# A five-layer transformer kernel: modulation vectors by a multiply-and-sum along rows of 1024 on VectorE instead of sums over partitions

## What is computed

```python
c_act = jax.nn.silu(c)
for i in range(DEPTH):
    mod = c_act @ ada_w[i] + ada_b[i]                    # [1024] @ [1024, 6144]
    sh1, sc1, g1, sh2, sc2, g2 = jnp.split(mod, 6, axis=-1)
    h = modulate(rmsnorm(x, norm_gain[i, 0]), sh1, sc1)
    y = mixer(h)                                         # swa, gla or fox
    x = x + g1[:, None, :] * y
    h = modulate(rmsnorm(x, norm_gain[i, 1]), sh2, sc2)
    x = x + g2[:, None, :] * swiglu(h, ffn_w_gu[i], ffn_w_down[i])
```

## Time and profile before

| | us |
|---|---|
| median of 3 runs | 1900.2 |
| lowest, highest | 1897.8, 1906.18 |
| span of the profiled execution (first to last instruction) | 1892.6 |
| median less that span | 7.6 |
| PE busy in the profiled execution | 1724.5 |
| DVE busy | 1362.8 |
| ACT busy | 813.9 |
| POOL busy | 630.0 |
| mean granted clock of PE, of full speed | 0.924 |

### The profile page before, as it was taken

One profiled execution on the slowest core, in us unless ns is written; L12 is line 12 of the kernel. 1 busy time (PEld: TensorE's weight loads), 2 busy tenths in 40 slices (PEclk: granted clock), 3 DMA queues, 4 the chain that ended last, 5 costly groups with the idle time before them and its releaser, 6 DMA issues.

```text
span 1892.6 us, 32608 instructions
## 1 busy us (share of the span) xinstructions
PE 1724.5 (91%) x12934; PEld 1603.9 (85%) x12934; DVE 1362.8 (72%) x1665; ACT 813.9 (43%) x1113; POOL 630.0 (33%) x268
## 2 busy tenths in 40 slices
PE   2868899989899999899999998989999898799998
PEld 2836899989789999897699998859999787489998
DVE  6886899986647999843259998855999854535554
ACT  2333444445534433443343443454344355445453
POOL 0112244532102544321224544133454314314433
PEclk9967899989889999897599999969999999799999
DMA  9642588764314876642048876404887635125551
GB/s 351 263 142 84 223 352 305 275 266 163 129 67 189 350 291 259 255 168 89 1 157 333 300 293 241 164 1 156 331 309 291 242 136 190 34 95 178 193 179 44
DMA packets 53937, 382.71 MB, mean 202 GB/s; under 512 B 6224, under 2 KB 6480, under 8 KB 8160
## 3 DMA queue, kind: packets, MB, share of 16 engines
q1 hardware_dynamic: 51840, 375.23, 52.6%
q0 software_dynamic: 2016, 6.36, 1.0%
HBM read 377.37 MB, written 4.19 MB: 202 GB/s over the span
## 4 chain that ended last, share of the span: by engine, by line
issue 40%; PE 31%; POOL 17%; DVE 7%; ACT 3%; DMA 1%; POOLq 0%; DVEq 0%; SPq 0%; ACTq 0%
PE PS L1369 17%; POOL wlo L681 10%; PE PS L1388 4%; POOL alo L748 4%; POOL acc_parts L756 3%; PE PS L1522 2%; DVE acc L1032 2%; PE PS L1414 1%; PE PS L1568 1%; DVE SCR L1222 1%; DVE NM L1226 1%; ACT SCR L915 1%; DMA adar<-ada 1%; ACT whi L777 1%; PE PS L1547 1%
## 5 line engine op out<-in xcount | busy, mean ns | idle before, releaser
L1369 PE MATMUL PS<-hhi,whi 128*128 128x256 f32 x2624 | 754.3, 287 | 19.8 <-DVE hlo L1067 18.5
L1369 PE MATMUL PS<-hlo,whi 128*128 128x256 f32 x2624 | 749.3, 286 | 0.0
L1369 PE MATMUL PS<-hhi,wlo 128*128 128x256 f32 x2624 | 749.1, 285 | 0.0
L777 ACT ACTIVATE whi<-raw 128x2048 fp32r<-128x2048 f32 x234 | 446.4, 1910 | 286.9 <-PE PS L1369 237.3
L1369 PEld LDWEIGHTS PS<-hhi,whi 128*128 128x128 f32 x2624 | 510.7, 195 | 33.5 <-issue 30.4
L1369 PEld LDWEIGHTS PS<-hlo,whi 128*128 128x128 f32 x2624 | 510.5, 195 | 2.5 <-issue 1.0
L1369 PEld LDWEIGHTS PS<-hhi,wlo 128*128 128x128 f32 x2624 | 510.5, 195 | 0.0
L681 POOL TENSOR_TENSOR wlo<-raw,whi 128x2048 fp32r<-128x2048 f32 x76 | 355.6, 4678 | 409.8 <-ACT whi L777 409.8
L1016 DVE TENSOR_TENSOR wlo<-raw,whi 128x2048 fp32r<-128x2048 f32 x158 | 364.1, 2304 | 162.3 <-ACT whi L777 162.1
L1032 DVE SCALAR_TENSOR_TENSOR acc<-adar,CC,acc 128x512 f32<-128x512 f32 x420 | 351.5, 837 | 13.8 <-DMA adar<-ada 0.3
L748 POOL TENSOR_TENSOR alo<-SCR,ahi 128x512 fp32r<-128x512 f32 x55 | 145.0, 2636 | 568.2 <-ACT ahi L977 568.2
(11 more groups left out here) (206 smaller groups left out, 1864.5 us busy)
## 6 DMA issues: line engine op xcount, KB each, us to landing
raw<-weights SPq DMA_DIRECT2D x234, 1024.0 KB, 6.7
adar<-ada SPq DMA_DIRECT2D x120, 1024.0 KB, 4.9
bias_rows<-acc POOLq DMA_DIRECT2D x12, 256.0 KB, 3.7
adar<-bias_rows POOLq DMA_DIRECT2D x8, 256.0 KB, 4.7
CST<-cst_in SPq DMA_DIRECT2D x1, 1064.0 KB, 9.1
X<-x_in SPq DMA_DIRECT2D x1, 1024.0 KB, 6.9
adar<-bias_rows POOLq DMA_DIRECT2D x8, 128.0 KB, 2.4
out_x<-X SPq DMA_DIRECT2D x1, 1024.0 KB, 3.9
```

What stands on the lines that cost most here:

```text
L777: act.activation(whi[:, u % CV, :], raw[:, u % RAW, :], ACT.Copy).then_inc(hi_done, 1)
L1369: m = pe.matmul(o, w(a), h(b), start=first and k_ == 0, stop=last and k_ == 2, skip_group_check=True)
```

## The change

The host lays the modulation matrix out the other way: a unit of 512 outputs is now four blocks of 128 outputs, with an output on each partition and its 1024 weights along the row. `CB` [128, 1024] holds the vector `c` on every partition (one DMA that reads the same 4 KB for each partition), and ACT takes its SiLU in place. DVE then needs one instruction for each block of 128 outputs, which multiplies the row by `CB` and gives the sum of the products (tensor_tensor_reduce, compiled to a main instruction and a second one that writes the sum to `AS`), and one that adds the bias to four sums. `ada_turn` and its waits on PE, the rounding on ACT, the remainder on POOL, and the identity product and row sum on DVE are gone, in all layers. For `b2`, which has another `c`, SP loads `CB` again in layer four (behind a wait for all modulation sums of that layer), and ACT takes the SiLU once more ahead of that layer's feed-forward loop.

```diff
-            def ada_sum(a, h, par_, blk, first=False):
+            def ada_sum(a, h, par_):
                 v.wait_ge(ada_in[h], 16 * a + 16)
-                dst = acc[:, par_, :]
-                for k in range(4):
-                    w = adar[:, h, 512 * k:512 * k + 512]
-                    cc = CC[:, 8 * blk + 4 * h + k:8 * blk + 4 * h + k + 1]
-                    if h == 0 and k == 0:
-                        if not first:
-                            v.wait_ge(ada_t, a - 1)
-                        v.tensor_scalar(dst, w, cc, None, ALU.mult).then_inc(ada_acc, 1)
-                    else:
-                        v.wait_ge(ada_acc, 8 * a + 4 * h + k)
-                        v.scalar_tensor_tensor(out=dst, in0=w, scalar=cc, in1=dst, op0=ALU.mult, op1=ALU.add).then_inc(ada_acc, 1)
...
+                if h == 0 and not (isinstance(a, int) and a < 2):
+                    v.wait_ge(ada_mod, a - 1)
+                for j in range(2):
+                    w = adar[:, h, D * j:D * j + D]
+                    v.tensor_tensor_reduce(out=w, in0=w, in1=CB[:], scale=1.0, scalar=0.0, op0=ALU.mult, op1=ALU.add,
+                                           accum_out=AS[:, par_, 2 * h + j:2 * h + j + 1]).then_inc(ada_dot, 1)
+
+            def ada_add(a, par_, lp, col, bias_col):
+
+                v.wait_ge(ada_dot, 4 * a + 4)
+                v.tensor_tensor(MOD[:, lp, bass.ds(col, 4)], AS[:, par_, :], PAR[:, bass.ds(PAR_AT["ada_b"] + bias_col, 4)], ALU.add).then_inc(ada_mod, 1)
...
                         lo(f + 6 + 3 * st, add=i)
                         if more:
-                            a = a0 + st + 2 * i
-                            picked = acc[:, st, :].rearrange("p (a b) -> p a b", b=P)
...
-                            v.tensor_tensor(picked, bank[2][:].rearrange("p (a b) -> p a b", b=P), ident.unsqueeze(1).to_broadcast([P, 4, P]), ALU.mult).then_inc(ada_pick, 1)
...
-                            v.tensor_reduce(m, picked, AXX, ALU.add).then_inc(ada_pick, 1)
...
-                            v.tensor_tensor(m, m, PAR[:, bass.ds(PAR_AT["ada_b"] + 48 * (l + 1) + 4 * st + 8 * i, 4)], ALU.add).then_inc(ada_mod, 1)
+                            ada_add(a0 + st + 2 * i, st, (l + 1) % 2, 4 * st + 8 * i, 48 * (l + 1) + 4 * st + 8 * i)
...
                         down(f + 4 + 3 * st, st, i)
-                        if l + 1 < L:
-                            pe.wait_ge(ada_lo, 10 * l + st + 1 + 2 * i)
-                            pe.wait_ge(ada_mod, ADA_UNITS * (l + 1) + st + 2 * i)
-                            for part in range(2):
-                                m = pe.matmul(bank[2][:], ones_r[:, 0:1].to_broadcast([P, P]), acc_parts[:, part, :], start=part == 0, stop=part == 1)
-                            m.then_inc(ada_t, 1)
...
-                            if j == 1 and l + 1 < L:
-                                pool.wait_ge(ada_hi, 10 * l + st + 1 + 2 * i)
-                                pool.tensor_tensor(acc_parts[:, 1, :], acc[:, st, :], acc_parts[:, 0, :].bitcast(F32), ALU.subtract).then_inc(ada_lo, 1)
...
-                            act.activation(acc_parts[:, 0, :], acc[:, st, :], ACT.Copy).then_inc(ada_hi, 1)
...
-            act.activation(CC[:], par("c", 16), ACT.Silu).then_inc(pro_act, 1)
+            act.activation(CB[:], CB[:], ACT.Silu).then_inc(c_act, 1)
...
+            sp.dma_start(CB[:], bass.AP(tensor=c_in.tensor, offset=0, ap=[[0, P], [1, D]])).then_inc(c_in_s, 16)
             sp.dma_start(PAR[:], par_in).then_inc(par_in_s, 16)
...
+                if more_b2(l):
+                    sp.wait_ge(ada_dot, 4 * ADA_UNITS * (l + 1))
+                    sp.dma_start(CB[:], bass.AP(tensor=c_in.tensor, offset=D, ap=[[0, P], [1, D]])).then_inc(c_in_s, 16)
```

109 lines of the change are left out of this document (34 added, 75 removed).

## The result

The changed kernel takes 1849.4 us (median of 4 runs, 1847.86 to 1851.46), the one before 1899.14 (4 runs, 1897.8 to 1906.18). The ratio is 0.973 (95% interval 0.9711 to 0.9749): faster by 2.7%. The forecast was 1846, in 1822 to 1880.

A forecast was written before the change was run, and what follows sets the result against it. PE was taken as the bound, with DVE also at its limit. Gains of 18 + 28 + 3.6 + 5 - 0.5 = 54 us took the 1892.6 span to 1838.5; plus 7.6 gave 1846, range 1822 to 1880.

The forecast's parts named there:

- Two limits in the loop: Feed-forward loop, layers one to four: PE's step of 17.73 us binds, DVE's 17.67 is right under it.
- The new instruction: DVE's multiply-and-sum of 1024 columns: priced as a plain product, 1.35 us a pair, between 1.15 and 2.5.
- DVE in a step: Feed-forward loop after the change: DVE needs 10.8 us, or 16.7 with all POOL waits, under PE's 17.28.
- The rival's threshold of 1.6 us a pair: Slow-pair rival, chance 0.14: from 1.6 us a pair DVE's loop step passes PE's of before; price 2050.
- The rival's second price: Slow-pair rival, chance 0.14, pair at 2.5 us: about 1985 us if only half of POOL's time collides, otherwise 2089.
- PE in the loop and the loop's end: Layers one to four: 18 us from PE's shorter steps, 28 from idle time and low clock behind the loops.
- Layer one: Its attention stage and projections, where DVE sets the pace: units 0.5 us shorter, together 5 us, bounds 0 and 14.
- Prologue: Before layer one: 1.2 us from shorter sums against 1.2 for loading `CB`; zero, within -2 and +3.
- Narrow products of layers two to five: Input projections: removing `ada_turn` saves PE 0.9 us a layer, 3.6 in all.
- From the span to the median: Whole kernel: 7.6 us between profiled span and median added to the predicted span of 1838.5.

The follow-up runs named there:

- b_narrow: Kernel before, with PE's two modulation matmuls in each feed-forward step writing 4 columns instead of 512, DVE's work kept: 1900.3 us, ratio 1.001.
- a_peback: Changed kernel with PE's two matmuls of 512 columns put back in each feed-forward step of layers one to four, results unread: 1865.4 us.
- b_nopick: Kernel before without DVE's identity product and row sum in the feed-forward loop, PE's matmuls kept: 1879.3 us, ratio 0.9901.
- a_waits: Changed kernel with PE's waits for the modulation sums put back in layer one and the prologue, without the narrow products: 1846.7 us.
- a_l0_long: Changed kernel with one more multiply-and-sum pair on DVE for each of modulation units 4 to 11 in layer one's attention part: 1861.5 us.
- a_pro: Changed kernel with halves of modulation units 1 to 3 also loaded into three free weight buffers in the prologue: 1840.9 us, ratio 0.9699.
- a_narrow4: Changed kernel with sixteen one-column products added on PE in the input projections of each of layers two to five: 1874.8 us, ratio 0.9859.

## Why the prediction was right

- *Two limits in the loop.* Right, and shown from both sides: b_narrow (no gain from PE alone), a_peback (16 us for PE's products once DVE has room), b_nopick (DVE's lag).
- *The new instruction.* The kind was right (a product of that width, not a scan), the size not: 1.15 us a pair where 1.35 was taken, the lower end. The accumulator's read overlaps with the next instruction nearly whole (start to start 1.14, durations 1.22 and 0.08).
- *DVE in a step.* 16.7 was the sum, with all of POOL's time added and 5.4 for the pairs. Measured 15.3: 0.8 less for the pairs, 0.3 because neighbours overlap (2.20 from start to start where 2.28 was counted), and 0.3 because POOL's time cost 5.6 and not 5.9. The wait for a load in the step above (2.34 us) saves nothing: POOL's wlo holds the pair up to 620.7 either way. The rival's threshold of 1.6 us a pair was a little low: two more pairs, that is 6 x 1.15 / 4 = 1.7 us, brought the time to 1894 us, about that of the kernel before, and 2.3 us brought 1978. The rival's second price doesn't follow from its own terms: with half of POOL's 5.9 us the step is 18.35, and the same sum gives about 1971, not 1985.
- *PE in the loop and the loop's end.* 46 predicted for four layers, 45.2 measured; 28 of the 46 for the loop's end, 28.5 measured by a_peback. The chain of whi, wlo and alo came as counted: the value unit ends at 391.90 - 5.76 = 386.1 us, and alo ends 5.6 behind it, where 5.5 was the sum. DVE's own lateness (L1310 at 387.03, 0.9 late, 1.1 counted) stands beside ScalarE's whi (386.34 to 388.25) and costs nothing. ScalarE's squares are what is late next, by 0.72 us in layer one and 0.46 to 0.50 in the others, where 0.6 was counted.
- *Layer one.* 5 predicted, 9.7 measured. The mis-sized term is the length of a modulation unit on VectorE: it was to become 0.5 us shorter, and it became 1.3 shorter (6.06 us of multiply-adds before, 7.31 to 13.37 us in the prologue; 4.73 for four pairs, 9.40 to 14.13). Eight units at 1.3 are 10.6. From the first product of one stage to that of the next, the input projections are 3.4 us shorter, the attention jobs 5.0, the output projections 1.4, where 1, 2 and 2 were predicted. One row of before suggests another account, a wait of PE in the input projections that the prediction did not price, with the narrow products behind it:

```profile
73.60 1.86 PE L1428 MATMUL PS<-CST,acc 128*128 128x1 f32 x8 [3.60 <-DVE acc L1032]
```

  But a_waits put that wait back, and the first job came no later: PE's wait is made up ahead of the job, DVE's pace is not (a_l0_long). The own time of the narrow products in layer one was not tested.
- *Prologue.* 0 predicted, +3.3 measured, just outside its bounds of -2 and +3 (with the spread of the starts above, 1.4 to 5.5). The 2.1 us by which `CB` delays the first pair (9.40 instead of 7.31) were counted as 1.2, and the 1.2 that the shorter sums were to give back did not come: the distance of the units is the round trip of the loads (9.5 to 10.1 us where it was 9.2), as a_pro shows. And the delay grows on its way to the weights of unit 1: SP issues their load 1.2 us later than before (31.95, not 30.75), and it lands 4.0 later (41.79, not 37.77). Why it took longer to land was not tested.
- *Narrow products of layers two to five.* 3.6 predicted, and in the two traces these parts are 3.5 us longer. The price is confirmed by a_narrow4, the gain is not visible: what failed is to count it as if the clock of these parts stayed as it was. The four parts together are at the lower level for 164 us before and for 182 in the changed kernel; which change brings that about stays open.
- *From the span to the median.* 7.6 us were added, and the sum of the parts was 7.7 us too large; the two errors cancelled for the most part. In all timed executions 1.8 to 1.9 us lie around the span (1848.01 to 1846.2), so the other 5.8 were the distance of one good execution of the kernel before to its median. That the forecast came within 4 us is luck. Without it the forecast would have been 1840, 9 us below the measured time; the direction and the range don't hang on it.

## What to carry to other kernels

A second engine whose step is just under that of the limiting one looks harmless. Here it was 0.06 us under: the lag with which it entered the loop of ten steps was not made up and came due behind the last step, 5.87 us with a low clock on top. With 0.37 us a step too much the same place and the steps together cost 45 us; with 0.8 us a step to spare nothing was lost. So ask for each loop how late the second engine enters it and how many steps it needs to catch up. And before an engine's work is cut, ask which engine stands right behind it: cutting half of the time of two matmuls brought 0 us in one kernel, and the whole of it was worth 16 in the other.

## What the runs showed of the hardware

- A multiply with a sum along the row over 1024 columns of fp32, both inputs in SBUF, takes 1221 ns (median of 240) and its accumulator's read 81, which overlaps with the next instruction; that is as fast as the product alone (1224).
- The duration of a small instruction on VectorE can be the rest of one on GpSimd: an addition of 4 columns in the loop takes 1.26 us beside GpSimd's remainder and 0.16 elsewhere; a pair takes up to 5.7.
- PE's clock can fall to 1.2 GHz while PE issues products without a pause, if they have one column each: 32 of them fill 421.89 to 426.48 us in a_narrow4, and the clock is 0.50 from 424.2 on.
- The same code can take longer in one execution than in the next, with the clock: 159.9 us at a mean of 0.76 and 165.4 at 0.72 for layer one up to its feed-forward part.
